# Down and output projections of a conformer decoder step: five float32r matmuls a k tile for six

## Chip, cores and metric

One core of one Trainium2 chip. The metric is the device time of one launch in microseconds; three runs of the kernel before are given, and one execution recorded by the profiler. TensorE is the matmul engine (PE in the rows, PEld its weight loads), VectorE is DVE, ScalarE is ACT, GpSimd is POOL, SyncE is SP.

## The reference

One step of a single-layer hybrid decoder for 512 prompt tokens and 8 sample tokens (each its own sequence), width 1024, all float32:

```
x = x + 0.5 * gt1 * swiglu(modulate(rms_norm(x), sh1, sc1), ffn1_gate, ffn1_up, ffn1_down)
h = modulate(rms_norm(x), sh2, sc2);  z = h @ w_in
y_conv = silu(layer_norm(depthwise conv of ca * sigmoid(cb))) @ w_conv_out
y_gla  = (rms_norm(gated linear attention(q, k, v, log_a)) * silu(r)) @ w_gla_out
merged = sigmoid(g_conv) * y_conv + sigmoid(g_gla) * y_gla
x = x + gt2 * (merged @ w_out)
x = x + 0.5 * gt3 * swiglu(modulate(rms_norm(x), sh3, sc3), ffn2_gate, ffn2_up, ffn2_down)
y = modulate(rms_norm(x), shf, scf)
```

where swiglu(h) = (silu(h @ w_gate) * (h @ w_up)) @ w_down, with a hidden width of 2816 = 22 tiles of 128. gt1 to gt3 differ by sequence, so a prompt token has one gate column and the 8 sample tokens have 8.

## The kernel before

Activations lie transposed: 128 channels on the partitions, a tile of 128 channels by N = 520 tokens (512 prompt, 8 sample). To keep float32 accuracy with the one-pass float32r type, each weight and each activation is split into a high part (rounded to float32r) and a low part (the rest), and a product is high x high + high x low + low x high, added up in PSUM.

The work of TensorE is cut into *units*: one output tile of 128 channels for all 520 tokens. `unit` (L629 to L647) runs over the k tiles (8, or 6 in the first down group) and issues for each of them six matmuls: three products, each in two halves of HALF = 260 tokens, into `pu[p][:, 0, 0:260]` and `pu[p][:, 1, 0:260]`, two PSUM banks. p alternates, so two units have four banks. Before a unit TensorE waits until the low part of its weights is ready (`s_lo`) and until unit n - 2 has been read from PSUM (`s_evac[p]`); after it, it signals `s_done`.

On `s_done` of unit n ScalarE casts the high part of the weights of unit n + 2 (L1227), and VectorE then makes the low part (`step`, L1680) and reads the result of unit n. For the down projections and the output projection that is `residual` (L1834 to L1845): two scalar_tensor_tensor operations, one for each bank, multiply the sum by the gate column and add it to x (260 tokens, and 252 prompt tokens); a small operation multiplies the 8 sample tokens by their gates (L1843) and releases the PSUM banks; the last one adds them to x (L1845) and tells ScalarE that the tile of x is ready (`s_x`).

A feed-forward net is done in three groups of 6, 8 and 8 hidden tiles. Group 0: ordinary up and gate units, then 8 down units with 6 k tiles. Groups 1 and 2: gate and up products by a scheme of seven block products, 11 weight blocks a turn, four turns (`product`, L812 on, and `up_unit`), then 8 down units with 8 k tiles. During down units 5 to 7 of groups 0 and 1 VectorE also adds up weight blocks (L1960) and makes the low parts of the first four blocks of the next group (L1969); in group 0 it further forms and splits sums of h (L1938, L1947). Sequence of block products: P1, P2 into the banks of `pu[0]`, which unit 6 used, then P6, P5 into those of `pu[1]`, which unit 7 used: `sums_of_blocks` waits for `s_evac[1]` before P6.

After group 2, and after the output projection, comes a normalisation: ScalarE squares each tile of x when `s_x` says so (L1266), VectorE adds the squares up, TensorE sums over the partitions (L726; in the final one L893), and scale, shift and splits follow before the next unit.

Other users of float32r on TensorE: all up, gate, in, conv and output units (L646, L660, L817, L828; 260 columns) and the outer products of the sample keys (L1098, 256 columns). Plain float32 matmuls (L726, L1064, L709, L753) are recorded as two instructions each.

The order on each engine is written out by hand; between engines only semaphores act.

Of the kernel before, what the change touches and what calls it, by code (L numbers as in the profile page):

```python
# [18 lines left out]
F32 = mybir.dt.float32  # L19
# [12 lines left out]
N = NP + NS  # L32
HALF = N // 2
FF = 2816
TAPS = 31
# [111 lines left out]
def decoder_step(nc, a, o):  # L147
# [3 lines left out]
    with ExitStack() as ctx:  # L151
        def sb(name, shape, dt=F32):
            return ctx.enter_context(nc.sbuf_tensor(name, shape, dt))
# [30 lines left out]
        assert off <= BF  # L184
        f_hl = []
        with ExitStack() as c2:
            for nm in ("f_hi", "f_lo"):
                f_hl.append(c2.enter_context(nc.sbuf_tensor(nm, [P, KT, N], F32R)))
        f_hi, f_lo = f_hl
        work = sb("work", [P, BF])  # L190

# [43 lines left out]
        c_f = sb("c_f", [P, KT, CG])  # L235
        t8 = sb("t8", [P, 2, NS])
        hs = sb("hs", [P, KT, NS])
# [103 lines left out]
        s_cpy = sem("state_conv_copied")  # L341
        s_xsp, s_xr = sem("x_rows_spilled"), sem("x_rows_restored")

# [26 lines left out]
        s_ys, s_yst, s_yc = sem("sample_y_scaled"), sem("sample_y_transposed"), sem("y_chunk_ready")  # L370
        s_shd, s_shl = sem("shift_rows_stored"), sem("shifts_spread")
        s_dv, s_ac = sem("dve_step"), sem("act_step")

# [105 lines left out]
        def _(pool):  # L479
# [132 lines left out]
            pool.wait_ge(s_xsp, 16)  # L612
            pool.dma_start(x_rows, x_rows_d).then_inc(s_xr, 16)
            pool.wait_ge(s_done, at["out"])
# [10 lines left out]
        def _(pe):  # L625
# [7 lines left out]
            def unit(n, p, hi, lo, k_tiles=KT, ready=None, done=1):  # L633


                weights_and_psum(n, p)
                for k in range(k_tiles):
                    if ready is not None:
                        s, v, first = ready
                        if k == 0 and first > 1:  # L640
                            pe.wait_ge(s, v + first)
                        elif k >= first or k == 0:
                            pe.wait_ge(s, v + k + 1)
                    for j, (w, m) in enumerate(((w_hi, hi), (w_hi, lo), (w_lo, hi))):
# [3 lines left out]
                last.then_inc(s_done, done)  # L648

            def unit_pair(n, hi, lo, s, v, between=None, together=KT):  # L650
# [246 lines left out]
            def ffn(which):  # L897
# [12 lines left out]
                for g in range(3):  # L910
# [21 lines left out]
                    if which == 2 and g == 2:  # L932
                        for c in range(KT):
                            if c < 2:
                                pe.wait_ge(s_um, 2 * TURNS * (2 * (which - 1) + g) - 1 + c)
                            unit(Lin(at["down2_2"] + c), c % 2, f_hi, f_lo, GROUPS[g],
                                 ready=(s_a, a0, GROUPS[g] - 1) if c == 0 else None)
                            if c:
                                y_transposes(c - 1)
                        continue  # L940
                    with pe.Fori(0, 2) as i:
                        for c in range(4):
                            if g and c < 2:
                                pe.wait_ge(s_um, 2 * TURNS * (2 * (which - 1) + g) - 1 + c)
                            unit(Lin(at[f"down{which}_{g}"] + c, 4, i), c % 2, f_hi, f_lo, GROUPS[g],
                                 ready=(s_a, a0, GROUPS[g] - 1) if c == 0 else None)
                            ada_part(c, ADA_DOWN[g], i)
# [253 lines left out]
            for name, hi, lo, s, v in (("ygla", o_hi, o_lo, s_osp, 0),  # L1201
                                       ("out", h_hi, h_lo, s_mp, 0)):
                with pe.Fori(0, 2) as i:
                    for c in range(4):
                        unit(Lin(at[name] + c, 4, i), c % 2, hi, lo, ready=(s, v, 1) if c == 0 else None)
            norm_sums(3)
# [461 lines left out]
        def _(dve):  # L1668
# [164 lines left out]

            def residual(n, m, gt):  # L1834

                p = n.base % 2
                g = lambda a, b: flat(mod[:, bass.ds(m + 8 * gt, 1), a:b])
                ps = pu[p]
                V.scalar_tensor_tensor(tile(x, m, 0, HALF), ps[:, 0, 0:HALF], g(0, 1), tile(x, m, 0, HALF),
                                       ALU.mult, ALU.add)  # L1840
                V.scalar_tensor_tensor(tile(x, m, HALF, NP), ps[:, 1, 0:NP - HALF], g(0, 1), tile(x, m, HALF, NP),
                                       ALU.mult, ALU.add)
                V.tensor_tensor(t8[:, p, :], ps[:, 1, NP - HALF:HALF], g(1, 9), ALU.mult).then_inc(s_evac[p], 1)  # L1843
                dve.wait_ge(s_evac[p], n.half().value(1, 1))
                V.tensor_tensor(tile(x, m, NP, N), tile(x, m, NP, N), t8[:, p, :], ALU.add).then_inc(s_x, 1)  # L1845


            def last_residual(n, m, gt, more=True):

                dve.wait_ge(s_done, n.value(1, 1))  # L1850
                residual(n, m, gt)
                if more:
                    step(n)
# [166 lines left out]
            def ffn(which, gt):  # L2020
# [32 lines left out]
                for g in range(3):  # L2053
# [3 lines left out]
                    for c in range(KT - (g == 2)):  # L2057
# [6 lines left out]
                        else:  # L2064
                            step(n, n0 + c + 2 < UNITS)
                        residual(n, c, gt)
                        if which == 2 and g == 2:
# [14 lines left out]
                    if g == 2:  # L2082
                        add_square(q, Lin(KT - 2))
                        last_square(q)
                        last_residual(Lin(n0 + KT - 1), KT - 1, gt, n0 + KT + 1 < UNITS)
                        if which == 2:
                            y_samples(KT - 1)
# [341 lines left out]
            with dve.Fori(0, 2) as i:  # L2429
                for c in range(4):  # L2430
# [10 lines left out]
                    V.tensor_tensor(tile(h_lo, t), s, tile(h_hi, t).bitcast(F32), ALU.subtract).then_inc(s_mp, 1)  # L2441
            dve.wait_ge(s_xr, 16)
            for i, k in bodies(dve, 2, 1):
                for c in range(4):
                    n = Lin(at["out"] + 4 * k + c, 4, i)
                    if c == 3 and i is not None:
                        add_square(3, Lin(KT - 2))
                        last_square(3)
                        last_residual(n, Lin(4 * k + c, 4, i).value(), GT2)
                        continue  # L2450
                    step(n)
                    residual(n, Lin(4 * k + c, 4, i).value(), GT2)
                    if i is not None or c:
# [53 lines left out]
```

## Time and profile before

| | us |
|---|---|
| median of 3 runs | 1432.65 (1431.9 to 1434.09) |
| span of the profiled execution | 1432.1 |
| TensorE busy | 1389.1 (97%) |
| VectorE busy | 977.2 (68%) |
| ScalarE busy | 539.3 (38%) |

The profiled execution's own time is given by its span, first to last instruction; no other figure of that execution stands beside the runs. Matmuls are pipelined and the recorded time of one (about 0.28 us for 260 columns) overlaps the next ones, so the pace is read from starts: of a row that merges n matmuls, (time of the row - time of one) / (n - 1). Granted clock 1.00 means 2.4 GHz, 0.5 means 1.2 GHz.

### The profile page before, as it was taken

Reading aid. Unit: us, or ns where it says so; the run is one execution under the profiler, and the core shown is the slowest. Engines: PE = TensorE matmul, PEld = TensorE weight load, DVE = VectorE, ACT = ScalarE, POOL = GpSimd, SP = SyncE. Lnnn points to the kernel's source line nnn. Section 1 sums busy time; section 2 is a strip of 40 time slices with the busy share of each in tenths; the row PEclk is TensorE's granted clock in tenths of the full one; section 3 lists DMA queues with packets and bytes.
Section 4 is the critical chain, followed back from the end, with each engine's and each line's share of the span. In section 5 each row is a group of like instructions: output and inputs, shape, how many; then the busy total and the mean of one; then the engine's idle time right before and its main releaser. Section 6 shows DMA issues by size and latency. Waiting matters only on the chain.

```text
span 1432.1 us, 28796 instructions
## 1 busy us (share of the span) xinstructions
PE 1389.1 (97%) x11782; PEld 1344.0 (94%) x11782; DVE 977.2 (68%) x1731; ACT 539.3 (38%) x797; POOL 80.2 (6%) x120
## 2 busy tenths in 40 slices
PE   6999999999999999999999999999999999999996
PEld 5899999999998999999899897999899999999996
DVE  6446675357547588998998997854554776456745
ACT  5423343224336222524243237422352344224433
POOL 6100000010001000000000000100000000000000
PEclk9999999999999999999999999999999999999998
DMA  9754646454364223213334453626312332323321
GB/s 322 237 177 155 205 149 206 147 168 142 103 208 142 89 88 93 89 60 104 125 128 146 136 169 127 220 91 198 104 59 74 92 117 89 114 76 106 101 77 60
DMA packets 132701, 189.49 MB, mean 132 GB/s; under 512 B 4621, under 2 KB 112545, under 8 KB 132386
## 3 DMA queue, kind: packets, MB, share of 16 engines
q1 hardware_dynamic: 111388, 112.54, 25.0%
q0 software_dynamic: 17136, 66.87, 14.0%
q10 hardware_dynamic: 4070, 8.57, 1.6%
q8 instruction: 77, 1.26, 0.4%
q14 instruction: 30, 0.25, 0.1%
HBM read 173.73 MB, written 15.18 MB: 132 GB/s over the span
## 4 chain that ended last, share of the span: by engine, by line
PE 84%; DVE 10%; ACT 3%; issue 2%; DMA 1%; POOL 0%; DVEq 0%; ACTq 0%
PE pu L646 51%; PE pu L828 13%; PE pu L817 11%; PE pu L660 2%; PE pg L690 2%; DVE w_lo L1680 1%; DMA work<-in_w_ada 1%; PE pg L1064 1%; ACT w_hi L1227 1%; DVE d L2106 1%; DVE w_lo L1969 1%; DVE work L2216 1%; PE pg L726 0%; DVE work L2215 0%; DVE work L2227 0%
## 5 line engine op out<-in xcount | busy, mean ns | idle before, releaser
L1680 DVE TENSOR_TENSOR w_lo<-raw,w_hi 128x1024 fp32r<-128x1024 f32 x152 | 186.1, 1225 | 255.5 <-ACT w_hi L1227 255.4
L1227 ACT CAST w_hi<-raw 128x1024 fp32r<-128x1024 f32 x152 | 158.9, 1046 | 412.0 <-PE pu L646 373.0
L646 PE MATMUL pu<-h_hi,w_hi 128*128 128x260 f32 x1408 | 288.4, 286 | 4.6 <-DVE work L2381 2.8
L646 PE MATMUL pu<-h_hi,w_lo 128*128 128x260 f32 x1408 | 284.1, 283 | 0.0
L646 PE MATMUL pu<-h_lo,w_hi 128*128 128x260 f32 x1408 | 283.3, 283 | 0.0
L646 PEld LDWEIGHTS pu<-h_hi,w_hi 128*128 128x128 f32 x1408 | 217.7, 189 | 8.7 <-DVE w_lo L1680 4.8
L646 PEld LDWEIGHTS pu<-h_hi,w_lo 128*128 128x128 f32 x1408 | 217.4, 189 | 0.0
L646 PEld LDWEIGHTS pu<-h_lo,w_hi 128*128 128x128 f32 x1408 | 217.2, 189 | 0.0
L2106 DVE SCALAR_TENSOR_TENSOR d<-u,cw,d 128x512 f32<-128x512 f32 x240 | 163.2, 745 | 0.1
L646 PE MATMUL pu<-f_hi,w_hi 128*128 128x260 f32 x704 | 142.9, 284 | 0.0
L646 PE MATMUL pu<-f_hi,w_lo 128*128 128x260 f32 x704 | 141.8, 283 | 0.0
L646 PE MATMUL pu<-f_lo,w_hi 128*128 128x260 f32 x704 | 141.3, 282 | 0.0
L1346 ACT CAST w_hi<-raw 128x512 fp32r<-128x512 f32 x112 | 69.1, 620 | 123.7 <-PE pu L817 70.8
L646 PEld LDWEIGHTS pu<-f_hi,w_hi 128*128 128x128 f32 x704 | 108.4, 188 | 2.0 <-issue 1.9
L646 PEld LDWEIGHTS pu<-f_hi,w_lo 128*128 128x128 f32 x704 | 108.4, 188 | 0.0
L646 PEld LDWEIGHTS pu<-f_lo,w_hi 128*128 128x128 f32 x704 | 108.2, 188 | 0.0
L828 PE MATMUL pu<-h_hi,w_hi 128*128 128x260 f32 x512 | 103.5, 283 | 0.0
L828 PE MATMUL pu<-h_hi,w_lo 128*128 128x260 f32 x512 | 103.0, 283 | 0.0
L828 PE MATMUL pu<-h_lo,w_hi 128*128 128x260 f32 x512 | 102.9, 282 | 0.0
L1969 DVE TENSOR_TENSOR w_lo<-raw,w_hi 128x512 fp32r<-128x512 f32 x112 | 77.2, 692 | 20.0 <-ACT w_hi L1346 18.1
L828 PEld LDWEIGHTS pu<-h_hi,w_lo 128*128 128x128 f32 x512 | 78.8, 188 | 0.0
L828 PEld LDWEIGHTS pu<-h_lo,w_hi 128*128 128x128 f32 x512 | 78.8, 188 | 0.0
(352 smaller groups left out, 2369.7 us busy)
## 6 DMA issues: line engine op xcount, KB each, us to landing
raw_a<-in_w_ada POOLq DMA_DIRECT2D x30, 1024.0 KB, 7.9
raw<-in_w_in SPq DMA_DIRECT2D x28, 1024.0 KB, 5.2
raw<-in_ffn_up SPq DMA_DIRECT2D x22, 1024.0 KB, 5.3
raw<-in_ffn_gate SPq DMA_DIRECT2D x21, 1024.0 KB, 5.3
raw<-in_ffn_down SPq DMA_DIRECT2D x16, 1024.0 KB, 5.1
gates_d<-sg ACTq DMA_DIRECT2D x24, 260.0 KB, 2.4
raw<-in_ffn_down SPq DMA_DIRECT2D x8, 768.0 KB, 4.4
work<-gates_d POOLq DMA_DIRECT2D x2, 2080.0 KB, 8.8
```

What stands on the lines that cost most here:

```text
L646: last = mm(pu[p][:, e, 0:HALF], w[p][:, k, :], m[:, k, e * HALF:(e + 1) * HALF], start=(k == 0 and j == 0), stop=(k == k_tiles - 1 and j ...
L660: last = mm(pu[p][:, e, 0:HALF], w[p][:, k, :], m[:, k, e * HALF:(e + 1) * HALF], start=(k == 0 and j == 0), stop=(k == KT - 1 and j == 2))
L690: last = mm(ps[CG * g:CG * (g + 1), bank, c:c + 256], c_f[:, k, :], src[:, k, :], start=(k < 4), stop=(k >= 4), tile_position=(0, CG * g))
L817: last = mm(bank, w_block(w, j)[:, k, :], m[:, k, :], start=(k == 0 and n == 0), stop=(k == 3 and n == 2))
L828: last = mm(pu[p][:, e, 0:HALF], w_block(w, j + half)[:, k, :], m[:, 4 * half + k, e * HALF:(e + 1) * HALF], start=(half == 0 and k == 0 a ...
L1064: last = mm(pg[:, l % 2, c * CH:(c + 1) * CH], m, m if rhs is None else rhs[:, c * CH:(c + 1) * CH], start=True, stop=True)
L1227: nc.scalar.copy(w_hi[p][:], raw[:, slot, :, p * P:(p + 1) * P]).then_inc(s_hi, 1)
L1346: nc.scalar.copy(w_block(w_hi, j), src).then_inc(s_bhi, 1)
L1680: V.tensor_tensor(w_lo[p][:], raw[:, slot, :, p * P:(p + 1) * P], w_hi[p][:].bitcast(F32), ALU.subtract).then_inc(s_lo, 1)
L1969: V.tensor_tensor(w_block(w_lo, j), src, w_block(w_hi, j).bitcast(F32), ALU.subtract).then_inc(s_blo, 1)
L2106: conv.mark(V.scalar_tensor_tensor(d[:, t, 0:NP], flat(u[:, t:t + 1, bass.ds(tap + s, NP)]), cw[:, bass.ds((tap + s) * KT + t, 1)], d[:, t ...
L2216: V.tensor_tensor(e[:, :, 0, :], mid, b[:, :, 0, :], ALU.subtract).then_inc(s_gd, 1)
```

## The change

The high and low parts of an activation become two slices of one tensor (`h2`, `f2`), and down units and output units use a new function, `unit_uneven`. It splits the 520 tokens into LEFT = 276 and REST = 244. In each k tile the 276 tokens get three matmuls (high x high, high x low, low x high) into bank 0; the high and low part of the 244 tokens are streamed by one matmul of 488 columns against the high part of the weights, into two sums of 244 columns beside each other in bank 1; and the low part of the weights meets the high part of the 244 tokens in a matmul of 244 columns that is added to the first of these sums. The other units stay as they are.

`residual` has one more sum to add: the 236 prompt tokens of bank 1 twice, from the first and from the second sum, and 2 x 8 sample tokens, whose two products are added together before they go to x. Three of its operations now wait for earlier ones of the same engine by a semaphore `s_res`. The PSUM banks are released by the third large operation.

```diff
+LEFT = 276
+REST = N - LEFT
-        h_hi = sb("h_hi", [P, KT, N], F32R)
-        h_lo = sb("h_lo", [P, KT, N], F32R)
+        h2 = sb("h2", [P, 2, KT, N], F32R)
+        h_hi, h_lo = h2[:, 0], h2[:, 1]
...
+        f2, work = overlay(("f2", [P, 2, KT, N], F32R), ("work", [P, BF], F32))
+        f_hi, f_lo = f2[:, 0], f2[:, 1]
...
-        t8 = sb("t8", [P, 2, NS])
+        t8 = sb("t8", [P, 2, 2, NS])
...
+            def unit_uneven(n, p, both, k_tiles=KT, ready=None):
+                weights_and_psum(n, p)
+                hi, lo = both[:, 0], both[:, 1]
+                left, rest = pu[p][:, 0, 0:LEFT], pu[p][:, 1, 0:2 * REST]
+                for k in range(k_tiles):
...
+                    start, stop = k == 0, k == k_tiles - 1
+                    mm(left, w_hi[p][:, k, :], hi[:, k, 0:LEFT], start=start, stop=False)
+                    mm(rest.rearrange("p (s n) -> p s n", s=2), w_hi[p][:, k, :], both[:, :, k, LEFT:N],
+                       start=start, stop=False)
+                    mm(left, w_hi[p][:, k, :], lo[:, k, 0:LEFT], start=False, stop=False)
+                    mm(left, w_lo[p][:, k, :], hi[:, k, 0:LEFT], start=False, stop=stop)
+                    last = mm(rest[:, 0:REST], w_lo[p][:, k, :], hi[:, k, LEFT:N], start=False, stop=stop)
+                last.then_inc(s_done, 1)
...
-                            unit(Lin(at[f"down{which}_{g}"] + c, 4, i), c % 2, f_hi, f_lo, GROUPS[g],
-                                 ready=(s_a, a0, GROUPS[g] - 1) if c == 0 else None)
+                            unit_uneven(Lin(at[f"down{which}_{g}"] + c, 4, i), c % 2, f2, GROUPS[g],
+                                        ready=(s_a, a0, GROUPS[g] - 1) if c == 0 else None)
...
+            with pe.Fori(0, 2) as i:
+                for c in range(4):
+                    unit_uneven(Lin(at["out"] + c, 4, i), c % 2, h2, ready=(s_mp, 0, 1) if c == 0 else None)
...
-            def residual(n, m, gt):
+            def residual(n, m, gt, r):
                 p = n.base % 2
                 g = lambda a, b: flat(mod[:, bass.ds(m + 8 * gt, 1), a:b])
...
+                left, hi, lo = pu[p][:, 0, 0:LEFT], pu[p][:, 1, 0:NP - LEFT], pu[p][:, 1, REST:REST + NP - LEFT]
+                samples = pu[p][:, 1, 0:2 * REST].rearrange("p (s n) -> p s n", s=2)[:, :, NP - LEFT:REST]
+                V.scalar_tensor_tensor(tile(x, m, LEFT, NP), hi, g(0, 1), tile(x, m, LEFT, NP), ALU.mult, ALU.add
+                                       ).then_inc(s_res, 1)
+                V.scalar_tensor_tensor(tile(x, m, 0, LEFT), left, g(0, 1), tile(x, m, 0, LEFT), ALU.mult, ALU.add)
+                V.tensor_tensor(t8[:, p], samples, g(1, 9).unsqueeze(1).to_broadcast([P, 2, NS]), ALU.mult
+                                ).then_inc(s_res, 1)
+                dve.wait_ge(s_res, r.value(3, 1))
+                V.scalar_tensor_tensor(tile(x, m, LEFT, NP), lo, g(0, 1), tile(x, m, LEFT, NP), ALU.mult, ALU.add
+                                       ).then_inc(s_evac[p], 1)
+                dve.wait_ge(s_res, r.value(3, 2))
+                V.tensor_tensor(t8[:, p, 0, :], t8[:, p, 0, :], t8[:, p, 1, :], ALU.add).then_inc(s_res, 1)
+                dve.wait_ge(s_res, r.value(3, 3))
+                V.tensor_tensor(tile(x, m, NP, N), tile(x, m, NP, N), t8[:, p, 0, :], ALU.add).then_inc(s_x, 1)
```

Beside this, the two semaphores for the spill and the reload of the x rows become one, with a wait for 32 in place of 16 on the second.

## Rows read from the trace of the kernel before

**Rows 1.** The page: engines' share of the span, granted clock, chain by engine.

```profile
PE 1389.1 (97%) x11782; PEld 1344.0 (94%) x11782; DVE 977.2 (68%) x1731; ACT 539.3 (38%) x797; POOL 80.2 (6%) x120
...
PEclk9999999999999999999999999999999999999998
...
PE 84%; DVE 10%; ACT 3%; issue 2%; DMA 1%; POOL 0%; DVEq 0%; ACTq 0%
```

**Rows 2.** The chain of waits in order of time (start us, us, what), two down stages.

```profile
393.27 46.15 PE pu L646 x384
...
1235.09 46.15 PE pu L646 x384
```

**Rows 3.** Timeline of TensorE and its weight loads (start us, us, engine, what).

```profile
692.88 0.64 PE L1098 MATMUL pg<-kv 96*128 96x256 f32 x4
...
1030.17 1.04 PE L726 MATMUL pg<-sg,ones 128*128 128x260 f32 x4
...
1037.81 1.86 PEld L709 LDWEIGHTS pg<-sel,lb 128*128 128x128 f32 x16 [1.25 <-DVE sg L1763]
...
686.14 0.97 PEld L1064 LDWEIGHTS pg<-work 128*128 128x128 f32 x8 [0.52 <-issue]
...
1041.44 0.64 PE L660 MATMUL pu<-h_hi,w_hi 128*128 128x260 f32 x2
1041.87 0.64 PE L660 MATMUL pu<-h_lo,w_hi 128*128 128x260 f32 x2
```

**Rows 4.** Windows: stretch, span, busy us of each engine, granted clock, DMA share, GB/s.

```profile
393.00:439.00 46.00, 46.00 (x385) 46.00 (x384) 22.40 (x45) 14.67 (x17) 3.57 (x4) 1.00 0.58 184
1235.00:1281.00 46.00, 46.00 (x385) 46.00 (x384) 21.09 (x44) 9.00 (x10) 0.00 (x0) 1.00 0.29 92
```

**Rows 5.** Groups of VectorE instructions: count, busy us, mean ns, idle before.

```profile
L1839 DVE SCALAR_TENSOR_TENSOR x<-pu,mod,x 128x260 f32<-128x260 f32 x56 | 27.0, 482 | 7.0 <-PE pu L646 7.0
L1841 DVE SCALAR_TENSOR_TENSOR x<-pu,mod,x 128x252 f32<-128x252 f32 x56 | 26.4, 471 | 0.0
```

**Rows 6.** Timeline of VectorE in down group 0 of the second network.

```profile
1140.92 1.23 DVE L1680 TENSOR_TENSOR w_lo<-raw,w_hi 128x1024 fp32r<-128x1024 f32 x1 [0.85 <-ACT w_hi L1227]
1142.07 0.48 DVE L1839 SCALAR_TENSOR_TENSOR x<-pu,mod,x 128x260 f32<-128x260 f32 x1
1142.47 0.47 DVE L1841 SCALAR_TENSOR_TENSOR x<-pu,mod,x 128x252 f32<-128x252 f32 x1
1142.85 0.16 DVE L1843 TENSOR_TENSOR t<-pu,mod 128x8 f32<-128x8 f32 x1
1143.04 0.17 DVE L1845 TENSOR_TENSOR x<-x,t 128x8 f32<-128x8 f32 x1
1143.13 0.69 DVE L1960 TENSOR_TENSOR w_sums<-raw 128x512 f32<-128x512 f32 x1
```

**Rows 7.** The chain at the end of that group.

```profile
1149.20 1.29 DVE w_lo L1969 x2
1150.49 0.40 DVE x L1839
1150.89 0.39 DVE x L1841
1151.28 0.08 DVE t L1843
...
1151.40 7.45 PE pu L817 x60
```

**Rows 8.** The chain at the end of the output units.

```profile
1031.36 0.18 DVE x L1845
...
1031.62 0.64 ACT sg L1266
...
1032.31 1.16 PE pg L726 x4
```

**Rows 9.** Who waited for the release of the PSUM banks, L1843 (us, times).

```profile
  PEld pu L817: 1.9, 4
```

More of the change, by code:

```diff
@@ L184, in decoder_step @@
         assert off <= BF
[L185 to L190, printed above, removed]
+        f2, work = overlay(("f2", [P, 2, KT, N], F32R), ("work", [P, BF], F32))
+        f_hi, f_lo = f2[:, 0], f2[:, 1]
         def wk(name):
@@ L371, in decoder_step @@
         s_shd, s_shl = sem("shift_rows_stored"), sem("shifts_spread")
+        s_res = sem("residual_step")
         s_dv, s_ac = sem("dve_step"), sem("act_step")
@@ L612, in _ @@
             pool.wait_ge(s_xsp, 16)
-            pool.dma_start(x_rows, x_rows_d).then_inc(s_xr, 16)
+            pool.dma_start(x_rows, x_rows_d).then_inc(s_xsp, 16)
             pool.wait_ge(s_done, at["out"])
@@ L648, in unit @@
                 last.then_inc(s_done, done)
+            def unit_uneven(n, p, both, k_tiles=KT, ready=None):
[3 more added lines that the diff above has]
+                for k in range(k_tiles):
+                    if ready is not None:
+                        s, v, first = ready
+                        if k == 0 and first > 1:
+                            pe.wait_ge(s, v + first)
+                        elif k >= first or k == 0:
+                            pe.wait_ge(s, v + k + 1)
+                    start, stop = k == 0, k == k_tiles - 1
[6 more added lines that the diff above has]
+                last.then_inc(s_done, 1)
             def unit_pair(n, hi, lo, s, v, between=None, together=KT):
@@ L935, in ffn @@
                                 pe.wait_ge(s_um, 2 * TURNS * (2 * (which - 1) + g) - 1 + c)
-                            unit(Lin(at["down2_2"] + c), c % 2, f_hi, f_lo, GROUPS[g],
-                                 ready=(s_a, a0, GROUPS[g] - 1) if c == 0 else None)
+                            unit_uneven(Lin(at["down2_2"] + c), c % 2, f2, GROUPS[g],
+                                        ready=(s_a, a0, GROUPS[g] - 1) if c == 0 else None)
                             if c:
@@ L1200, in _ @@
                     unit(Lin(at["yconv"] + 4 + c, 4, i), c % 2, h_hi, h_lo)
[L1201 to L1205, printed above, removed]
+            with pe.Fori(0, 2) as i:
+                for c in range(4):
+                    unit(Lin(at["ygla"] + c, 4, i), c % 2, o_hi, o_lo, ready=(s_osp, 0, 1) if c == 0 else None)
+            with pe.Fori(0, 2) as i:
+                for c in range(4):
+                    unit_uneven(Lin(at["out"] + c, 4, i), c % 2, h2, ready=(s_mp, 0, 1) if c == 0 else None)
             norm_sums(3)
@@ L1850, in last_residual @@
+                dve.wait_ge(s_res, r.value(3, 3))
+                V.tensor_tensor(tile(x, m, NP, N), tile(x, m, NP, N), t8[:, p, 0, :], ALU.add).then_inc(s_x, 1)
+            def last_residual(n, m, gt, r, more=True):
                 dve.wait_ge(s_done, n.value(1, 1))
-                residual(n, m, gt)
+                residual(n, m, gt, r)
                 if more:
@@ L2065, in ffn @@
                             step(n, n0 + c + 2 < UNITS)
-                        residual(n, c, gt)
+                        residual(n, c, gt, Lin((which - 1) * 4 * KT + 8 * g + c))
                         if which == 2 and g == 2:
@@ L2084, in ffn @@
                         last_square(q)
-                        last_residual(Lin(n0 + KT - 1), KT - 1, gt, n0 + KT + 1 < UNITS)
+                        last_residual(Lin(n0 + KT - 1), KT - 1, gt, Lin((which - 1) * 4 * KT + 3 * KT - 1), n0 + KT + 1 < UNITS)
                         if which == 2:
@@ L2448, in _ @@
                         last_square(3)
-                        last_residual(n, Lin(4 * k + c, 4, i).value(), GT2)
+                        last_residual(n, Lin(4 * k + c, 4, i).value(), GT2, Lin(4 * k + c + 3 * KT, 4, i))
                         continue
                     step(n)
-                    residual(n, Lin(4 * k + c, 4, i).value(), GT2)
+                    residual(n, Lin(4 * k + c, 4, i).value(), GT2, Lin(4 * k + c + 3 * KT, 4, i))
                     if i is not None or c:
```

15 lines of the change are left out of this document (3 added, 12 removed).

## The prediction

> **What bounds the kernel now.** I read the page's first part, then the chain of waits, then single stretches. TensorE is busy 97% of the span and stands on 84% of the chain, at full clock except in a few short stretches [rows 1]. In a down stage the reader sees one piece of 384 matmuls in 46.15 us [rows 2]: 120.2 ns each, no wait in between, while VectorE is busy 21 to 22 of 46 us [rows 4]. So in most units that change, TensorE's own pace decides, and the question is what a matmul costs by its width.
>
> A 260-column stream at 2.4 GHz is 108.3 ns, and the pace is 11.9 ns above it. The plain float32 matmul of the same width (recorded as two instructions) runs (1.04 - 0.38) / 3 = 219 ns apart, for 2 x 108.3 = 216.7 ns of columns: only 2.4 above [rows 3]. Weight loads alone, behind 10-column matmuls, follow at (1.86 - 0.19) / 15 = 111 ns, behind 128-column float32 ones at (0.97 - 0.19) / 7 = 111 too. At half clock the 260-column float32r matmul takes 0.435 / 2 = 217 ns, its bare columns [rows 3]. And the one float32r form of another width, 256 columns, runs at (0.64 - 0.28) / 3 = 120 ns: four columns less and no visible gain, within the 10 ns grain of that row [rows 3]. A stream of 111 ns (columns plus 2.4) and a load of 111 ns or a little more go on side by side, and the pair comes out at 120: I read it as a floor that each load sets, with little of it depending on the columns.
>
> **The change on TensorE.** A k tile has 6 x 260 = 1560 columns before, and 276 x 3 + 488 + 244 = 1560 after. No column is saved; one instruction with its load is. It concerns 2 x (6 + 8 + 8) x 8 = 352 k tiles of down units and 64 of out units, 416 in all.
> - Before: 6 x 120.2 = 721.2 ns.
> - The 276-column matmul: stream 115 + 2.4 = 117.4, still under 120.2. Lower bound 117.4, upper bound 115 + 11.9 = 126.9 if all the excess is added whatever the width. I take 120.2, since it is nearest to the 256 against 260 comparison.
> - The 244-column one: between its stream of 101.7 + 2.4 = 104.1 and 120.2. I take the floor, 120.2. No float32r matmul under 256 columns stands in the trace; the upper end, if it went as plain float32, is a rival below.
> - The 488-column one: 203.3 + 2.4 = 205.7, by the 219 ns row, whose load is hidden in the same way; upper bound 203.3 + 11.9 = 215.2. I take 205.7. Its two pieces of 244 lie apart in SBUF; the strided operands elsewhere (products of h) keep the same pace, so I put nothing on that.
> - After: 4 x 120.2 + 205.7 = 686.5. Saved 34.7 ns, x 416 = 14.4 us.
>
> The Trainium skill ("TensorE: Matmul & The Clock Gate", section Back-to-back issue gap) gives columns / 2.4 + 2.5 ns for an isolated matmul, and warns that in a stream of pairs of load and matmul both set the spacing. By the bare formula six matmuls would take 665 ns and five 662.5, a saving of only 1.0 us in all, less than what VectorE costs below. The trace's 120 against the formula's 110.8 speaks for the warning and against the formula.
>
> **The change on VectorE.** A residual has now three scalar_tensor_tensor and three small operations, for two and two. In the chain the first two occupy 0.40 and 0.39 us, the small ones 0.08 and about 0.17 [rows 7, 8]. The third piece (236 columns) adds 0.38; the added 8-column sum, which waits for the one before it, adds about 0.2. So + 0.6 us until x is updated, x 56 residuals = 34 us more of VectorE. The PSUM release moves from behind the second large and one small operation to behind a third large one: start to start 0.39 + 0.41 + 0.19, then 0.45 to its end, 1.44 us against 0.94 [rows 5 to 7]: + 0.5. Bounds for each: + 0.3 (small ones hidden) and + 0.8 (each wait costing 0.1 more). The waits on s_res are for the engine's own earlier operations; behind them stand only the following residual and weight splits. Where this is hidden:
> - Down groups 1 and 2 and the out units: 5.5 us units after, VectorE work 3 to 4 us in each; hidden.
> - Down group 0: a unit shrinks from 4.31 to 4.10 us; its VectorE work (weight split, residual, one split or sum of h) leaves 0.85 us idle (the 1140.92 row of [rows 6]; five units look like it). 0.85 - 0.6 - 0.2 leaves about nothing, but the split of the next weights is due 1.7 us later, so TensorE does not wait inside.
>
> Where it is not:
> - The end of down group 0, twice. From the split at 1140.92 on VectorE has no pause, and the chain runs over it until the release of unit 7 lets the third block product start at 1151.40 [rows 6, 7]. Three residuals lie in that stretch: 0.6 + 0.6 + 0.5 = 1.7 us later, and TensorE's saving of units 6 and 7 (12 k tiles, 0.4 us) is lost too: 2.1 each, 4.2.
> - The end of down group 1, twice: the same product waits for the release, but VectorE had been idle before. 0.5 each, 1.0. In all four places the load of that product waits already, 1.9 us together [rows 9], so there is no slack to eat.
> - The end of down group 2 in both networks and of out: the last residual, ACT's square and the sums follow each other [rows 8]. 0.6 each, 1.8.
>
> Sum: 14.4 - 4.2 - 1.0 - 1.8 = 7.4 us less. DMA issues, ScalarE's casts and the joined semaphore of the x rows move nothing: a pair of down units still takes over 8 us, and the pieces of rows 2 show no wait for a load from memory.
>
> **From span to time.** The profiled execution has a span of 1432.1; the median of the runs is 1432.65, so what lies around it (and the spread of runs) is 0.5. 1432.1 - 7.4 + 0.5 = 1425.2 us.
>
> **The rivals.**
> - *The excess belongs to each matmul* (11.9 ns on every instruction, whatever its width). Saved 11.9 x 416 = 5.0 us; VectorE's costs are 2 x (1.7 + 0.14) + 1.0 + 1.8 = 6.5. Time 1434.1. For it: the excess vanishes at half clock, as a fixed cost hidden in a slower stream would. Against: the same fixed cost is only 2.4 in the float32 row, and the 256-column row shows no shorter time.
> - *Load and stream share a read path*, so that (columns + 128) sets the time: 276 columns 125.2, 244 columns 115.2, 488 stream-bound at 205.7. 696.5 a k tile, 10.3 us saved, 6.8 lost: 1429.1. It fits 120.2 and 111 at once, but not the 219 ns row, if that one reads as fast.
> - *Slower: columns are all that counts.* Place: the float32r stream itself, at 120.2 / 260 = 0.462 ns a column. Then nothing is saved, and the ends pay VectorE's 2 x 1.7 + 1.0 + 1.8 = 6.2: 1438.8. It decides from the point where the saving of a k tile is under 6.2 / 416 = 15 ns. For it: 256 columns would give 118.3, which that row can hardly tell from 120. Against: the half-clock row. The skill's bare formula ends at the same place (1437.8).
> - *Slower: a narrow float32r matmul is run like plain float32.* 244 columns would cost 2 x 219 x 244 / 260 = 411 ns instead of 120, 121 us over 416. VectorE's costs would then be covered, and the time about 1540. Nothing in the profile excludes it: 256 is the narrowest float32r width that stands there.
> - *It is not what it says*, that the matmul over two pieces splits into two at the engine: then six instructions stay and the case is as the columns one.
>
> **How the numbers follow.** Forecast (a floor by load) 0.53; shared path 0.13; excess a matmul 0.15; columns alone, or no real change of instructions, 0.09; narrow matmul slow 0.05; another size of the ends or of the floor 0.05, either way. A change of under 0.2% (2.9 us) can't be told from none here. The forecast and most of the shared path are faster, 0.62; the excess case and what is left of the shared path fall within, 0.22; the rest slower, 0.16. The forecast's own range is 1421.5 (residual at + 0.3) to 1429 (residual at + 0.8, 276 columns at 122). The whole range takes in the excess case and stops short of the columns one: 1421.5 to 1435.5. Two short half-clock stretches on the chain can also come or go, 1.5 us each (one of them is in [rows 3]: 16 matmuls, 97 ns more for each).
>
> **What would show it.** Eight down units of group 1 and 2 in about 43.9 us for 46.15 would be the floor; 45.4 the excess; 46.15 the columns. The starts in a k tile should be 120, 206, 120, 120, 120 apart. A residual of 1.65 us on VectorE; the third block product after group 0 waiting over 2 us instead of about 0.5; the last residual of out 0.6 longer. The forecast is wrong if the 276-column matmuls stand at 125 or more, or the 244-column one above 125.

## The result, and the profile after

The changed kernel takes 1438.35 us (median of 7 runs, 1435.63 to 1439.79), the kernel before 1433.46 (7 runs beside it, 1431.9 to 1434.09): ratio 1.0035, 95% interval 1.0024 to 1.0045. It is slower by 4.9 us, where 7.4 us less were forecast, and stands above the range. The case "columns are all that counts" gave 1438.8; how much of that agreement is luck is said below.

The page of the changed kernel, lines that answer to [rows 1]:

```profile
PE 1389.2 (97%) x11366; PEld 1329.6 (92%) x11366; DVE 1002.0 (70%) x1843; ACT 539.4 (38%) x797; POOL 80.0 (6%) x120
...
PEclk8999999999999999999999999999999999999998
...
PE 82%; DVE 11%; ACT 3%; DMA 2%; issue 2%; ACTq 0%; DVEq 0%; SPq 0%
```

416 matmuls are gone (11782 to 11366), and TensorE is busy as long as before: 1389.2 us for 1389.1. VectorE has 112 instructions more and 24.8 us more busy time, and 1% more of the chain of waits.

One down stage of the changed kernel, from the timeline of TensorE (start us, us, engine, what): its first matmul, one whole k tile and the next one's first, and the first matmul behind the stage. It answers to [rows 2].

```profile
396.30 0.29 PE L663 MATMUL pu<-f,w_hi 128*128 128x276 f32 x1
...
419.97 0.29 PE L663 MATMUL pu<-f,w_hi 128*128 128x276 f32 x1
420.10 0.38 PE L664 MATMUL pu<-f,w_hi 128*128 128x488 f32 x1
420.32 0.29 PE L666 MATMUL pu<-f,w_hi 128*128 128x276 f32 x1
420.44 0.29 PE L667 MATMUL pu<-f,w_lo 128*128 128x276 f32 x1
420.57 0.28 PE L668 MATMUL pu<-f,w_lo 128*128 128x244 f32 x1
420.68 0.29 PE L663 MATMUL pu<-f,w_hi 128*128 128x276 f32 x1
```

The next stage's first matmul starts at 442.22, so the stage takes 45.92 us, 0.2 less than the same eight units before [rows 2]: 717.5 ns a k tile for 721. The starts in a k tile are 130, 220, 120, 130, 110 ns apart in this row of 10 ns grain; over all recorded k tiles they are 128, 221.7, 125.6, 126.9 and 114.0, about 717 together (six matmuls took 720 before). Forecast were 120, 206, 120, 120, 120: the first, second and third kinds are all dearer, and the narrow one is cheaper than the floor that was assumed for it.

VectorE in the changed kernel, groups of the three large operations of a residual (count, busy us, mean ns, idle before), as [rows 5], and the last residual of down group 0 in the second network from the timeline (start us, us), as [rows 6]:

```profile
L1864 DVE SCALAR_TENSOR_TENSOR x<-pu,mod,x 128x276 f32<-128x276 f32 x56 | 27.8, 496 | 0.0
L1862 DVE SCALAR_TENSOR_TENSOR x<-pu,mod,x 128x236 f32<-128x236 f32 x56 | 25.6, 457 | 5.2 <-PE pu L668 5.2
L1868 DVE SCALAR_TENSOR_TENSOR x<-pu,mod,x 128x236 f32<-128x236 f32 x56 | 25.3, 452 | 0.0
```

```profile
1155.99 0.46 DVE L1862 SCALAR_TENSOR_TENSOR x<-pu,mod,x 128x236 f32<-128x236 f32 x1
1156.36 0.49 DVE L1864 SCALAR_TENSOR_TENSOR x<-pu,mod,x 128x276 f32<-128x276 f32 x1
1156.78 0.16 DVE L1865 TENSOR_TENSOR t<-pu,mod 128x16 f32<-128x16 f32 x1
1156.86 0.45 DVE L1868 SCALAR_TENSOR_TENSOR x<-pu,mod,x 128x236 f32<-128x236 f32 x1
1157.23 0.15 DVE L1871 TENSOR_TENSOR t<-t 128x8 f32<-128x8 f32 x1
1157.41 0.17 DVE L1873 TENSOR_TENSOR x<-x,t 128x8 f32<-128x8 f32 x1
```

From the first start to the end of L1868, which releases the banks, pass 1.32 us, for 0.94 before: + 0.4 (0.5 forecast). To the start of the next operation pass 1.5 us for 1.06 in [rows 6]: + 0.45 (0.6 forecast). The sum of 8 columns waits for the one before it, and 0.18 us lie between the two starts.

What this makes of the places without cover, first in the timeline of TensorE (in brackets the idle time before the instruction and who ended it), then among those who waited for L1868 (us, times), as [rows 9]:

```profile
1153.32 0.39 PE L838 MATMUL pu<-h,w_hi 128*128 128x260 f32 x1 [0.33 <-DVE x L1868]
...
1157.36 0.39 PE L838 MATMUL pu<-t_hi,w_hi 128*128 128x260 f32 x1 [0.89 <-DVE x L1868]
```

```profile
  PEld pu L838: 4.9, 5
  PE pu L838: 3.9, 5
```

Before, the first product of the next group had no wait of its own at the end of group 0, only P6 had; now P1 waits too (1153.32), and P6 starts 1.17 us after its predecessor where it took 0.53 before. This is the second network; in the first P1 has no wait, and P6 alone waits 1.12 us longer. The load that waited 1.9 us in four places waits 4.9 us in five.

### The profile page after: what moved, and what is told of

It reads as the page before. It is cut to its first block, busy times and chain, and to the rows that moved or that the text cites. A ratio compares the mean times of both kernels' runs of the same rounds, so it can differ in the third digit from the quotient of the medians.

```text
span 1438.0 us, 28076 instructions
## 1 busy us (share of the span) xinstructions
PE 1389.2 (97%) x11366; PEld 1329.6 (92%) x11366; DVE 1002.0 (70%) x1843; ACT 539.4 (38%) x797; POOL 80.0 (6%) x120
## 4 chain that ended last, share of the span: by engine, by line
PE 82%; DVE 11%; ACT 3%; DMA 2%; issue 2%; ACTq 0%; DVEq 0%; SPq 0%
PE pu L645 30%; PE pu L849 13%; PE pu L838 11%; PE pu L664 6%; PE pu L663 3%; PE pu L667 3%; PE pu L666 3%; PE pu L668 3%; PE pu L681 2%; PE pg L711 2%; DVE w_lo L1702 2%; DMA raw<-in_w_out 1%; ACT w_hi L1249 1%; PE pg L1085 1%; DVE d L2134 1%
## 5 line engine op out<-in xcount | busy, mean ns | idle before, releaser
L645 PE MATMUL pu<-h,w_hi 128*128 128x260 f32 x2560 | 416.1, 285 | 4.3 <-DVE work L2409 2.8
L645 PEld LDWEIGHTS pu<-h,w_hi 128*128 128x128 f32 x2560 | 352.1, 189 | 8.2 <-DVE w_lo L1702 4.9
L645 PE MATMUL pu<-h,w_lo 128*128 128x260 f32 x1280 | 258.3, 283 | 0.0
L645 PEld LDWEIGHTS pu<-h,w_lo 128*128 128x128 f32 x1280 | 197.8, 189 | 0.0
L849 PE MATMUL pu<-h,w_hi 128*128 128x260 f32 x1024 | 164.7, 283 | 0.0
L849 PEld LDWEIGHTS pu<-h,w_hi 128*128 128x128 f32 x1024 | 140.2, 188 | 0.0
L664 PE MATMUL pu<-f,w_hi 128*128 128x488 f32 x352 | 135.1, 384 | 0.0
L663 PE MATMUL pu<-f,w_hi 128*128 128x276 f32 x352 | 103.8, 295 | 0.0
L849 PE MATMUL pu<-h,w_lo 128*128 128x260 f32 x512 | 103.0, 283 | 0.0
L667 PE MATMUL pu<-f,w_lo 128*128 128x276 f32 x352 | 102.0, 290 | 0.0
L666 PE MATMUL pu<-f,w_hi 128*128 128x276 f32 x352 | 101.5, 288 | 0.0
L668 PE MATMUL pu<-f,w_lo 128*128 128x244 f32 x352 | 97.3, 276 | 0.0
L849 PEld LDWEIGHTS pu<-h,w_lo 128*128 128x128 f32 x512 | 78.8, 188 | 0.0
L838 PE MATMUL pu<-t_hi,w_hi 128*128 128x260 f32 x256 | 73.3, 286 | 3.6 <-DVE x L1868 3.6
L838 PE MATMUL pu<-t_lo,w_hi 128*128 128x260 f32 x256 | 73.4, 287 | 0.0
```

Of the source, the lines that this page charges most:

```text
L663: mm(left, w_hi[p][:, k, :], hi[:, k, 0:LEFT], start=start, stop=False)
L664: mm(rest.rearrange("p (s n) -> p s n", s=2), w_hi[p][:, k, :], both[:, :, k, LEFT:N], start=start, stop=False)
L666: mm(left, w_hi[p][:, k, :], lo[:, k, 0:LEFT], start=False, stop=False)
L667: mm(left, w_lo[p][:, k, :], hi[:, k, 0:LEFT], start=False, stop=stop)
L668: last = mm(rest[:, 0:REST], w_lo[p][:, k, :], hi[:, k, LEFT:N], start=False, stop=stop)
L838: last = mm(bank, w_block(w, j)[:, k, :], m[:, k, :], start=(k == 0 and n == 0), stop=(k == 3 and n == 2))
```

## The experiments

Ten further kernels were run. The first two split the change in its halves.

**e1_residual_only**: the kernel before, with the long residual. Short diff:

```diff
-                V.scalar_tensor_tensor(tile(x, m, 0, HALF), ps[:, 0, 0:HALF], g(0, 1), tile(x, m, 0, HALF),
-                                       ALU.mult, ALU.add)
...
+                dve.wait_ge(s_res, r.value(3, 1))
+                V.scalar_tensor_tensor(tile(x, m, HALF, NP), hi, g(0, 1), tile(x, m, HALF, NP), ALU.mult, ALU.add
+                                       ).then_inc(s_evac[p], 1)
+                dve.wait_ge(s_res, r.value(3, 2))
+                V.tensor_tensor(t8[:, p, 0, :], t8[:, p, 0, :], t8[:, p, 1, :], ALU.add).then_inc(s_res, 1)
```

> The kernel before with the longer residual alone: the second large operation is done twice (its sum is added twice, so this part of the output is another) and the sample pair is formed from both banks, so VectorE's work and waits are those of the changed kernel; TensorE keeps its six matmuls. Theory (the loss is VectorE's, at the ends): 4 to 6.5 us slower than before, so about 1438 to 1440, with the third block product after down group 0 waiting 1.1 to 1.7 us longer and the ends 0.4 to 0.5 us each; about 1.6 us of it is a half-clock stretch after the long stall at 159 us, if it comes. Rival (the loss is TensorE's, in the uneven units): within 1.5 us of before.

Measured: 1440.39 us (1440.12 to 1442.64), ratio 1.0052 (1.0038 to 1.0066). VectorE's part costs 7.0 us by the medians, a little more than the 4 to 6.5 that were expected, and covers the whole loss. The down stages keep their length; what grows are the stretches behind them. The waits of TensorE (total us, times, longest us), before, in this kernel, and in the changed one:

```profile
PE pg L726 <- ACT sg L1266: 2.2, 2, 1.1
PE pu L817 <- DVE t L1843: 0.9, 2, 0.6
```

```profile
PE pg L727 <- ACT sg L1267: 3.1, 2, 1.6
PE pu L818 <- DVE x L1847: 4.0, 5, 1.8
```

```profile
PE pg L747 <- ACT sg L1288: 3.0, 2, 1.5
PE pu L838 <- DVE x L1868: 3.9, 5, 1.7
```

The two with the long residual agree to 0.1 us, whatever TensorE does in between: two matmuls that open the sums of squares (+ 0.4 to 0.5 each) and the block products behind down groups 0 and 1 (3 us together).

**e2_uneven_old_residual**: the changed kernel with the short residual; the second sum of bank 1 is not added.

```diff
-                V.scalar_tensor_tensor(tile(x, m, LEFT, NP), lo, g(0, 1), tile(x, m, LEFT, NP), ALU.mult, ALU.add
-                                       ).then_inc(s_evac[p], 1)
...
+                V.tensor_tensor(t8[:, p, 0, :], ps[:, 1, NP - LEFT:REST], g(1, 9), ALU.mult).then_inc(s_evac[p], 1)
+                dve.wait_ge(s_evac[p], n.half().value(1, 1))
```

> The changed kernel with the short residual of before (two large and two small operations): the second sum (high weights x low part of 244 tokens) is left out of the output; TensorE does all that the change does. Theory (each matmul has its own excess, and the 488-column one 6.5 ns more): a k tile of 716 ns against 721, so 1 to 3 us faster than before. Rival (forecast of a floor, spoilt only by something that VectorE did): 10 us or more faster. Rival (uneven units are slower in themselves): not faster than before.

Measured: 1432.5 (1430.55 to 1434.35), ratio 0.9994 (0.9985 to 1.0003). In its trace the seven changed stages are together 0.95 us shorter than before, 2.3 ns a k tile over 416, where the forecast had 34.7. The waits at the ends are as before, 2.2 and 0.9 us. The other half of the change is thus worth about nothing: 1 to 3 us were expected, and the interval of the 0.9 us that the medians differ includes none. Ten and more, as a floor by load would give, are excluded, and + 7.0 and - 0.9 add up to the 4.9 of the change within their intervals.

What a matmul costs by its width is the open question, and the next ones ask it.

**e3_one_piece**: the 488 columns are read from one stretch of memory (the same number of columns of the high part alone).

```diff
-                    mm(rest.rearrange("p (s n) -> p s n", s=2), w_hi[p][:, k, :], both[:, :, k, LEFT:N],
+                    mm(rest, w_hi[p][:, k, :], hi[:, k, N - 2 * REST:N],
```

> The changed kernel with the 488-column matmul reading one contiguous run of 488 columns of the high part (tokens 32 to 520) instead of two pieces of 244; the products in both sums of bank 1 are other ones. Theory (a second piece of the operand costs 6 to 7 ns): the 488-column matmul goes from 221.7 to about 215 ns, start to start, all others stay. Rival (the excess grows with the width, 0.03 ns a column): it stays at 221 to 222.

Measured: 1438.02, one run. The 488 columns take 220.2 ns for 221.7, and the 244 after them 111.6 for 114.0; a k tile takes 714.1 ns for 716.7. By stage the gain is 0 to 4.8 ns a k tile: 2.8 in the stage shown above, 4.8 and 1.9 in the two of group 0, nothing in group 1 of the first network and group 2 of the second. The expected 6 to 7 ns are not there. So the second piece has at most a small price, and without it 220 remain against the 205.7 of the forecast.

**e4_left320**: another split.

```diff
-LEFT = 276
+LEFT = 320
```

> The changed kernel with 320 + 200 tokens instead of 276 + 244 (widths 320, 400, 320, 320, 200). Theory (columns / 2.4 plus about 12 ns for each matmul, the load only a lower limit of 111): 320 columns 145, the 400-column one 178.5 plus 6.5 = 185, 200 columns 111 to 113 instead of 95. The forecast's floor: 200 columns 120, 320 columns 136. Columns alone at 0.462 ns: 148, 185, 92.

Measured: 1445.26, one run. The timeline of TensorE:

```profile
420.78 0.25 PE L668 MATMUL pu<-f,w_lo 128*128 128x200 f32 x1
420.87 0.32 PE L663 MATMUL pu<-f,w_hi 128*128 128x320 f32 x1
421.03 0.34 PE L664 MATMUL pu<-f,w_hi 128*128 128x400 f32 x1
421.21 0.31 PE L666 MATMUL pu<-f,w_hi 128*128 128x320 f32 x1
```

From its start to the next one's the 200-column matmul takes 90 ns (93.9 on the mean): there is no floor at 120 for a single matmul and none at the 111 of a weight load. But the 320-column one behind it takes 166 ns, and the other two of that width 146.1 and 147.8: the 17 ns by which 200 columns stay under the load are given back on the next matmul, and 2 or 3 more. The load of the next weights thus still has to be paid, over two matmuls together.

**e10_left392**: the same further out, with 128 columns as the narrow one.

```diff
-LEFT = 276
+LEFT = 392
```

> The changed kernel with 392 + 128 tokens (widths 392, 256 in two pieces, 392, 392, 128). Theory: 392 columns 178.1, 256 in two pieces 118.5 to 121.5, and the 128-column one starts its successor after 62 to 66 ns, but what is missing to the weight load's 111 ns comes back on the next matmul (with 200 columns the next one stood at 166 for 146, 20 ns more), so 392 columns after it take 178 + 35 to 45. Rival (a floor at 111 or 120 for each matmul): 128 columns 111 or 120, and nothing on the next.

Measured: 1453.46, one run.

```profile
420.35 0.22 PE L668 MATMUL pu<-f,w_lo 128*128 128x128 f32 x1
420.41 0.40 PE L663 MATMUL pu<-f,w_hi 128*128 128x392 f32 x1
420.65 0.28 PE L664 MATMUL pu<-f,w_hi 128*128 128x256 f32 x1
420.77 0.34 PE L666 MATMUL pu<-f,w_hi 128*128 128x392 f32 x1
```

128 columns take 58.9 ns, 392 take 179.9 and 176.7, and the 392 behind the narrow one about 232: 52 ns under the load's 111, 54 given back. The 256 columns in two pieces take 118.0, no more than 256 in one piece in the next run. A narrow float32r matmul is run like any other here, so the rival of 411 ns has fallen; what narrowness costs is the load behind it.

**e9_left264_one**: 264 tokens on the left, and 512 contiguous columns on the right.

```diff
-LEFT = 276
+LEFT = 264
...
-                    mm(rest.rearrange("p (s n) -> p s n", s=2), w_hi[p][:, k, :], both[:, :, k, LEFT:N],
+                    mm(rest, w_hi[p][:, k, :], hi[:, k, N - 2 * REST:N],
```

> The changed kernel with 264 + 256 tokens, and the wide matmul (512 columns) reading one contiguous run of the high part (tokens 8 to 520), so its products are other ones. Theory (a float32r matmul takes 6.2 ns + 0.4385 ns a column, fitted on 200 to 488 columns): 264 columns 122.0, 512 columns 230.7, 256 columns 118.5; the k tile 715. Rival (a constant of 12 ns on columns / 2.4): 512 columns 225.3, 256 columns 118.7. The forecast's floor: 256 and 264 columns 120, 512 columns 216.

Measured: 1436.69, one run.

```profile
420.66 0.28 PE L663 MATMUL pu<-f,w_hi 128*128 128x264 f32 x1
420.78 0.40 PE L664 MATMUL pu<-f,w_hi 128*128 128x512 f32 x1
421.01 0.28 PE L666 MATMUL pu<-f,w_hi 128*128 128x264 f32 x1
...
421.26 0.28 PE L668 MATMUL pu<-f,w_lo 128*128 128x256 f32 x1
```

264 columns: 121.1 and 121.8 ns. 512: 233.4. 256: 118.3. The line that had been fitted to the widths from 200 to 488 columns is

time = 6.2 ns + 0.4385 ns x columns

| columns | measured, ns | by the line |
|---|---|---|
| 128 | 58.9 | 62.3 |
| 200 | 93.9 | 93.9 |
| 256 | 118.3 | 118.5 |
| 260 | 120.0 | 120.2 |
| 264 | 121.1, 121.8 | 122.0 |
| 320 | 146.1, 147.8 | 146.5 |
| 392 | 179.9, 176.7 | 178.1 |
| 488, one piece | 220.2 | 220.2 |
| 512 | 233.4 | 230.7 |

It fits the middle and misses both ends, 128 columns by 3.4 ns and 512 by 2.7, each the mean of over 300 matmuls. A line through all of them has a constant near 3 ns and a slope near 0.448. So the slope is well above the 0.4167 of bare columns in either fit, and the constant is small, but its size is not settled by the widths. The sum of a k tile gives it more directly, because its columns are 1560 in each form: six matmuls take 719.9 ns, five take 714.1 in e3_one_piece and 715.6 here. One instruction less is worth 5.8 or 4.3 ns, or 3.2 with the two pieces of the change (716.7).

Of the 11.9 ns that the forecast read above the columns of a 260-column matmul, roughly 4 to 6 thus belong to the instruction and the rest grows with the columns (5.7 by the slope of 0.4385). The Trainium skill ("TensorE: Matmul & The Clock Gate", section Back-to-back issue gap) has columns / 2.4 + 2.5 for an isolated matmul, 215.8 ns for 512 columns, and about 131 ns for a stream of pairs of load and matmul of that width. These runs show 233.4 and agree with neither.

**e5_load64**: the kernel before, with only 64 weight columns in the middle product, which makes its load shorter and leaves half of its output out.

```diff
-                            last = mm(pu[p][:, e, 0:HALF], w[p][:, k, :], m[:, k, e * HALF:(e + 1) * HALF],
+                            c = 64 if j == 1 else P
+                            last = mm(pu[p][0:c, e, 0:HALF], w[p][:, k, 0:c], m[:, k, e * HALF:(e + 1) * HALF],
```

> The kernel before, with the middle one of the three products (high weights x low part) made with 64 columns of weights instead of 128, for half of the channels only; its two loads are half as long. Theory S (what a matmul takes beyond 108.3 ns for 260 columns belongs to its stream, 6.2 ns for each and 5% on each column): all starts stay 120 apart. Rival L (it comes from the load beside it): the two matmuls during which a 64-column load runs go to about 111 to 114, the others stay at 120.

Measured: 1431.21, one run. The group of the shorter form (count, busy us, mean ns, idle before) and its loads:

```profile
L647 PE MATMUL pu<-h_lo,w_hi 128*64 128x260 f32 x1408 | 282.7, 282 | 0.0
...
L647 PEld LDWEIGHTS pu<-h_lo,w_hi 128*64 128x64 f32 x1408 | 179.1, 135 | 0.0
```

Its loads are recorded with 135 ns instead of 188, and six matmuls take 717.4 ns instead of 719.9; the matmuls with the short load take 118.0 and 119.7 ns for 118.9 and 120.3, and no other place in the k tile moves by more than 0.6 ns. If the load set the pace, two of the six would have gone to 111 to 114. So at 260 columns the excess is the stream's. Where its 5% a column and its few ns an instruction come from was not found.

**e6_two_pieces**: the kernel before, the middle product's 260 columns read as 2 x 130 from two places, to price a piece by itself.

```diff
+                            q = HALF // 2
+                            v = m[:, k, :].rearrange("p (a n) -> p a n", a=2)[:, :, e * q:(e + 1) * q]
+                            out = pu[p][:, e, 0:HALF].rearrange("p (a n) -> p a n", a=2)
```

> The kernel before, with the moving operand of the middle product of each half taken in two pieces of 130 columns, 260 apart, instead of one run of 260 (other tokens, so this product is another). Theory (a second piece costs 1.5 ns, as between 221.7 and 220.2 for 488 columns): these matmuls go from 120 to 121.5, the others stay. Rival (pieces cost nothing, the 1.5 ns was chance): 120 throughout. Rival (6 ns a piece, as first thought): 126.

Measured: 1434.15, one run. Two of six matmuls changed, and the six take 720.3 ns for 719.9. The two changed ones are up by 1.0 ns each, and the four others move by - 1.4 to + 0.9, so single places can't be read this finely. It does not give the 2.6 of e3; whether that is the distance of the pieces or their width stays open.

The last two undo the change at the ends, where VectorE has no cover.

**e8_short_end0**: the last three units of group 0, in both networks, as before (six matmuls and short residual), all else as changed.

```diff
+ENDS = (5, 8, 8, 8)
...
-                        residual(n, c, gt, Lin((which - 1) * 4 * KT + 8 * g + c))
+                        residual(n, c, gt, Lin((which - 1) * 4 * KT + 8 * g + c), c >= ENDS[g])
```

> As the run with short ends, but only at the end of down group 0 (units 5 to 7, both networks); the other ends keep the five matmuls and the long residual. Theory: what it wins over the changed kernel is the end of group 0, 1.1 us in each network, and the half-clock stretch of 1.6 us that follows the long stall at 160 us: 3 to 4 us, so 1434 to 1435. Rival (each end costs the same 0.4 us): under 1.5 us won, 1437 or more.

Measured: 1435.26 (1433.89 to 1436.15), ratio 1.0011 (1.0002 to 1.002), 3.1 us less than the change, where 3 to 4 were expected. Windows over the first network's end of group 0, first the changed kernel, then this one, last e9_left264_one over the same stretch of its own time (stretch, span, busy us of PE, PEld, DVE, ACT and POOL, granted clock, DMA share, GB/s), as [rows 4]:

```profile
155.00:161.00 6.00, 4.25 (x33) 3.88 (x32) 5.83 (x22) 2.66 (x5) 0.00 (x0) 1.00 0.00 0
161.00:164.40 3.40, 3.40 (x18) 3.40 (x17) 2.15 (x5) 0.62 (x1) 0.00 (x0) 0.50 0.23 36
```

```profile
155.00:161.00 6.00, 5.41 (x45) 5.20 (x45) 5.83 (x20) 2.66 (x5) 0.00 (x0) 1.00 0.01 4
161.00:164.40 3.40, 3.40 (x31) 3.40 (x30) 2.73 (x7) 1.24 (x2) 0.00 (x0) 1.00 0.30 60
```

```profile
155.16:161.16 6.00, 4.25 (x33) 3.85 (x32) 5.83 (x22) 2.66 (x5) 0.00 (x0) 1.00 0.00 0
161.16:164.56 3.40, 3.40 (x30) 3.40 (x30) 3.01 (x6) 1.13 (x2) 0.00 (x0) 1.00 0.20 31
```

VectorE is busy 5.83 of 6.00 us in all: the bound is there. In the changed kernel TensorE is busy 4.25 us of the six, and in the next 3.4 us the granted clock is 0.50, the lower of its two levels: 18 matmuls where the other kernel does 31. With the short ends TensorE was busy 5.41 us, and the clock stays. In this execution the extra pause thus costs twice: its own length, and 1.6 us of the half-clock stretch behind it. The pause does not always bring the lower clock. An idle time of about 1.75 us before P6 stands in four traces: in those of the change, of e1 and of e3 the half-clock stretch follows; in that of e9 TensorE was busy 4.25 of the six us as well, and the clock stayed at 1.00. No trace with a shorter idle time at this place (1.53 us in e4, 0.98 in e10, about 0.6 with the short residual) has the stretch.

**e7_short_ends**: the same, and also the last unit of groups 1 and 2 and of out.

```diff
+ENDS = (5, 7, 7, 7)
```

> The changed kernel, but the down units 5 to 7 of group 0, unit 7 of groups 1 and 2 and unit 7 of out go with six matmuls (276 and 244 tokens) and the short residual of two large operations. Theory (TensorE's gain is 4.6 ns for each of the 340 k tiles left, VectorE's cost is all at these ends): 1 to 2 us faster than the kernel before, 6 to 7 faster than the changed one, stalls at the ends as before. Rival (the longer residual also costs inside the stages): slower than before by 1 us or more.

Measured: 1432.76 (1431.7 to 1434.38), ratio 0.9996 (0.9987 to 1.0005), 5.6 us less than the change. The waits of TensorE here, then in e8_short_end0:

```profile
PE pg L758 <- ACT sg L1301: 2.3, 2, 1.2
...
PE pu L849 <- DVE t L1879: 0.6, 1, 0.6
```

```profile
PE pg L758 <- ACT sg L1301: 3.0, 2, 1.5
...
PE pu L849 <- DVE x L1891: 0.9, 2, 0.5
```

The two waits for L1891 behind group 1 are gone here; the single wait for L1879 behind group 0, 0.6 us, stands in both. All waits are back at those of the kernel before, or under them. Expected were 1 to 2 us less than before; measured are 0.8, with an interval that includes none. It is the best form of the change that was tried, and it can't be told from the kernel before.

## Why the prediction was wrong

The step that failed is the price of TensorE's matmuls, "After: 4 x 120.2 + 205.7 = 686.5. Saved 34.7 ns, x 416 = 14.4 us". Measured are 717 ns a k tile, and 0.95 us saved over all seven stages (read in e2, where no longer wait stands in them). Its terms:

- *276 columns, 120.2.* Measured 125.6 to 128; the line gives 127.2. It was the stated upper bound (126.9), and the sign by which the text would call itself wrong. Three of them: about + 20 ns. With that the reason given for it falls too, that the 256-column matmuls were no faster than the 260-column ones.
- *488 columns, 205.7.* Measured 221.7, and 220.2 in one piece; + 16. It lies even above the stated upper bound of 215.2, because the part that grows with the columns had been taken as fixed.
- *244 columns, 120.2.* Measured 114.0 (111.6 in e3): - 6. That this is less than 120.2 alone refutes the floor.
- *The two pieces, nothing.* About 2.6 ns a k tile by e3, of which the one saved instruction has only some 4 to 6 to give. In group 0 of the second network nothing is left of it: from the first start of the stage to the last 34.33 us before, 34.43 after; in that of the first network 39.34 and 39.20.

The reading behind it was "a floor that each load sets". Its supports did not carry it. The plain float32 row showed that *another* type, at twice the columns for each recorded instruction, stands 2.4 ns above them; the load row showed that loads can follow at 111, not that they lift 108 to 120; and the comparison of 256 with 260 columns, a difference of 1.7 ns when measured over many, was read in a row of 10 ns grain. e5 shortened the load without moving the pace; e4 and e10 went under it. Nor did the half-clock row exclude the columns' share: by it a 260-column matmul takes 217 ns, so an excess that only stands at full clock had been shown, not that it is fixed. "Columns are all that counts" (0.09) was nearest, in place and in time, though a few ns of each instruction are real. That its 1438.8 lies 0.45 us from the measured time is partly luck: it had 6.2 us at the ends, where 4.3 were found, and the half-clock stretch and the wait in the out units, which it did not have, make up for that. "The excess belongs to each matmul" has about half of it right (4 to 6 of 11.9), "shared path" gives 115.2 and 205.7 for 244 and 488 columns, and both miss 488.

**VectorE.** The mechanism and the places that were named were right, the sizes somewhat large, and one place that was called hidden was not (the out units, below). Forecast 7.0 us with the lost saving; the trace has:

| place | forecast | measured, us |
|---|---|---|
| end of group 0, net 1 | 2.1 | 1.12 |
| end of group 0, net 2 | 2.1 | 0.48 + 0.64 |
| end of group 1, twice | 1.0 | 0.37 + 0.38 |
| sums of squares after both group 2 and out | 1.8 | 0.39 + 0.45 + 0.45 |
| sum | 7.0 | 4.3 |

Group 0 was the mis-sized term. The added cost of a residual there is + 0.45 and not + 0.6, and the 0.4 us of lost saving do not exist where nothing is saved. In the second network the stall is shared by two waits, one of them at P1, which the text had not named. The chain at the end of out, as [rows 8]:

```profile
1034.53 0.47 DVE x L1862
1034.99 0.41 DVE x L1864
...
1035.49 0.37 DVE x L1868
...
1035.96 0.18 DVE x L1873
1036.22 0.65 ACT sg L1288
1036.91 1.16 PE pg L747 x4
```

The steps behind VectorE's last operation are as before (0.26 and 0.69 us from start to start, 0.26 and 0.69 in [rows 8]), so the whole addition is in the residual.

**What was not in the sum.** The half-clock stretch behind the first pause, 1.6 us; the text had it as a chance, "can also come or go", and not as what its own 1.7 us stall could bring. And a wait inside the out units, which the forecast called hidden. Their third block of weights takes long to arrive; the chain of waits of the changed kernel shows the transfer:

```profile
989.93 17.60 DMA raw<-in_w_out
```

Behind it come ScalarE's cast, VectorE's low part and the long residual, whose third large operation releases the banks for the fifth out unit at 1011.30. There 601 ns lie between two starts of TensorE, where about 120 are usual: 0.48 us. The transfer itself is not later than before (17.35 us in the kernel before, 17.53 in e2, and neither has a wait there). The wait stands in the traces of the change, of e3 (464 ns) and of e9 (545), which have the long residual in these units. It does not stand in e1, with the long residual and six matmuls, nor with the wider left parts of e4 and e10, nor in e7 and e8, where the transfer took 15.9 and 16.1 us. That the residual's added 0.4 us uses up a small reserve here is read from these traces; no run was made on it alone.

**The account** of the profiled executions, 1438.0 - 1432.1 = 5.9 us, from the starts of matching matmuls: TensorE's stages - 0.95; waits for VectorE + 4.3, and + 0.3 in the first block products at the end of group 0; half clock at 161 us + 1.6; the wait in the out units + 0.5; the start of the kernel + 0.4; small shifts elsewhere + 0.4; the end - 0.6. The last terms are no part of the change as far as the traces show: near 25 us the clock is at 0.50 for 10.2 us in place of 6.8, and at the end it falls to 0.50 later (at 1427.3 in place of 1419.6).

## What to carry to other kernels

Before an instruction is removed for its fixed cost, split the pace into the part per instruction and the part per column: several widths, timed over many matmuls, do it, and so does the sum of a group that has the same columns in fewer instructions (here 714 to 716 ns for 720); one comparison of neighbours in a coarse row does not. An excess is not fixed because it is small, and a row of another type does not price it. When TensorE's gain is paid with work on the engine that reads PSUM, price the last units of each stage first: nothing hides that work there, and a pause that it makes longer may bring the lower clock after it (here in three of four traces).

## What the runs showed of the hardware

- float32r matmuls of 128 rows and 128 weight columns, at granted clock 1.00, start 118.3 ns apart at 256 columns, 120.0 at 260, 146 to 148 at 320, 220.2 at 488 and 233.4 at 512: 0.44 to 0.45 ns a column and 3 to 6 ns an instruction.
- A matmul shorter than its weight load (111 ns) runs at its own pace, and the one behind it pays: + 20 ns behind 200 columns, + 54 behind 128.
- Reading one operand from two places cost 2.6 ns in a k tile of five matmuls (0 to 4.8 by stage), and 0.4 ns in a k tile in the other form that was tried.
- After 6.0 us with TensorE busy for 4.25, idle 1.75 us of it in one piece, the granted clock was 0.50 in the next 3.4 us in the trace of the change, and 1.00 in that of e9. After 5.41 busy of 6.0 at the same place (e8) it was 1.00.
